# One hybrid decoder layer: the q_b and k_b projections as one 2x2 block product of seven products

## The reference

```
h = rmsnorm(x, mix_norm_g)
u = h @ w_in                      # sections: q/k, v, o of the mLSTM; i, f gates; q, k, v of MoBA
ml_qk, ml_v, ml_o, ml_i, ml_f, mb_q, mb_k, mb_v = split(u)
...
q_b = rmsnorm(heads(mb_q), q_norm_g) * 64 ** -0.5     # per head of 64 columns
k_b = rmsnorm(heads(mb_k), k_norm_g)
h_b = moba_attention(q_b, k_b, v_b)
x = x + concat(h_m, h_b) @ w_out
x = x + moe_ffn(rmsnorm(x), ...)                      # 32 experts, clamped SwiGLU
x = x + sigmoid(rmsnorm(x) @ w_ple_gate) * (p @ w_ple_proj)
```

## Time and profile before

| | us |
|---|---|
| median of 3 runs (lowest, highest) | 1100.59 (1100.36, 1100.77) |
| the profiled execution | 1100.76 |
| its span, first to last instruction | 1099.0 |
| PE busy | 1069.6 (97%) |
| DVE, ACT, POOL busy | 265.5, 143.8, 35.7 |
| moved by DMA | 431.88 MB, mean 393 GB/s |

### The profile page before, as it was taken

One profiled execution on the slowest core, in us unless ns is written; L12 is line 12 of the kernel. 1 busy time (PEld: TensorE's weight loads), 2 busy tenths in 40 slices (PEclk: granted clock), 3 DMA queues, 4 the chain that ended last, 5 costly groups with the idle time before them and its releaser, 6 DMA issues.

```text
span 1099.0 us, 11965 instructions
## 1 busy us (share of the span) xinstructions
PE 1069.6 (97%) x5122; PEld 446.7 (41%) x5122; DVE 265.5 (24%) x535; ACT 143.8 (13%) x284; POOL 35.7 (3%) x52
## 2 busy tenths in 40 slices
PE   9999999999999999999999999998989899999998
PEld 5485563434343434343424333333343343433334
DVE  4285341232121212121211111121211021211122
ACT  4134350100000000000000000000000110000022
POOL 2421200000000000000000000000000000000000
PEclk9999999999999999999999999999999999999999
DMA  9943789999999999999999999999999999999981
GB/s 348 364 174 124 293 332 394 428 414 429 427 426 434 429 436 425 432 432 427 435 431 429 435 425 436 429 429 433 430 431 425 435 428 436 426 431 426 422 341 39
DMA packets 33788, 431.88 MB, mean 393 GB/s; under 512 B 5207, under 2 KB 5727, under 8 KB 16582
## 3 DMA queue, kind: packets, MB, share of 16 engines
q1 hardware_dynamic: 33520, 431.06, 93.2%
q10 hardware_dynamic: 214, 0.04, 0.0%
HBM read 430.04 MB, written 1.06 MB: 392 GB/s over the span
## 4 chain that ended last, share of the span: by engine, by line
PE 75%; DMA 23%; DVE 1%; issue 0%; ACT 0%; DVEq 0%; ACTq 0%
PE hu L1189 28%; DMA ring<-in_w_gate_up 20%; PE po L1219 16%; PE aux L1132 5%; PE aux L1140 3%; DMA ring<-in_w_down 3%; PE hu L792 3%; PE hu L1181 2%; PE hu L1000 2%; PE hu L808 2%; PE hu L798 2%; PE hu L834 1%; PE po L1196 1%; PE aux L1400 1%; PE aux L1165 1%; PE hu L1219 1%
## 5 line engine op out<-in xcount | busy, mean ns | idle before, releaser
L1189 PE MATMUL hu<-ring,num_xg 128*64 128x512 f32 x1920 | 438.4, 604 | 17.1 <-DMA ring<-in_w_gate_up 16.9
L1189 PEld LDWEIGHTS hu<-ring,num_xg 128*64 128x64 f32 x1920 | 132.8, 138 | 302.5 <-issue 273.2
L1219 PE MATMUL po<-ring,arena 128*64 128x512 f32 x976 | 216.2, 594 | 6.3 <-DMA ring<-in_w_down 6.3
L1219 PEld LDWEIGHTS po<-ring,arena 128*64 128x64 f32 x976 | 69.7, 137 | 147.9 <-issue 144.6
L1785 DVE TENSOR_SCALAR arena<-hu 128x512 f32<-128x512 f32 x31 | 21.4, 691 | 428.5 <-PE hu L1189 428.5
L1761 DVE TENSOR_TENSOR arena<-arena,aux 128x512 f32<-128x512 f32 x58 | 37.3, 684 | 131.7 <-PE aux L1140 119.9
L1132 PEld LDWEIGHTS aux<-num_xg,big 128*128 128x128 f32 x512 | 58.4, 192 | 13.0 <-issue 13.0
L1132 PE MATMUL aux<-num_xg,big 128*128 128x128 f32 x512 | 61.4, 278 | 0.0
L1774 DVE TENSOR_SCALAR arena<-iota_s,posm,gates 128x128 f32<-128x128 f32 x64 | 17.9, 342 | 118.2 <-PE po L1219 115.3
L2110 ACT ACTIVATE hu<-arena 128x512 f32<-128x512 f32 x31 | 18.6, 601 | 199.9 <-DVE arena L1785 199.9
L2126 ACT COPY arena<-po 128x512 f32<-128x512 f32 x16 | 9.4, 585 | 221.2 <-PE po L1209 221.2
(11 more groups left out here) (295 smaller groups left out, 670.8 us busy)
## 6 DMA issues: line engine op xcount, KB each, us to landing
ring<-in_w_gate_up SPq DMA_DIRECT2D x44, 4096.0 KB, 34.8
ring<-in_w_down SPq DMA_DIRECT2D x22, 4096.0 KB, 35.0
ring<-in_w_gate_up SPq DMA_DIRECT2D x37, 2048.0 KB, 14.5
ring<-in_w_down SPq DMA_DIRECT2D x14, 2048.0 KB, 15.9
ring<-in_w_in SPq DMA_DIRECT2D x6, 2048.0 KB, 16.2
ring<-in_w_down SPq DMA_DIRECT2D x8, 1024.0 KB, 31.5
ring<-in_w_gate_up SPq DMA_DIRECT2D x6, 1024.0 KB, 6.7
ring<-in_w_out SPq DMA_DIRECT2D x2, 2048.0 KB, 11.5
```

The lines of the kernel that those rows point to most:

```text
L1189: last = mm(hu[n * SLOTS:(n + 1) * SLOTS, 2 * e + b, :], rows_of[:, k, e * SLOTS:(e + 1) * SLOTS], features(w[:, o:o + D], n), start=first ...
L1219: last = mm(bank[n * SLOTS:(n + 1) * SLOTS, :], actT[:, f, h * SLOTS:(h + 1) * SLOTS], w[:, o:o + NB], start=(h == 0 and f == 0), stop=(h ...
```

## The change

Write the tokens as two tiles, and the contraction as two halves. The four blocks q_b and k_b of the two tiles become entries of one 2x2 block product. Its left factor is `raw_block(tt, half)`, its right one `qb_weights(half)`, `kb_weights(half)`. With four sums of row blocks s1 to s4 (POOL, 128x512) and four differences of weight blocks n1 (DVE), n2, n3, n4 (POOL, 128x2048), seven products of 4 steps give all four blocks. All seven read unscaled rows, so the row's factor now comes into the norms of all four blocks. The blocks are finished in the order q_b tile 0, k_b tile 0, k_b tile 1, q_b tile 1 (`BLOCKS`), by adds out of PSUM into `normed`, which ACT and DVE then read in place of the bank. n3 overwrites section 1's first half, n4 the place of n1. The row sums of the later block product (v, o) wait for the end of these products, the `scaled` pair is moved behind the gates, and the load of section 6 waits for n4.

```diff
+        n1 = ring[:, MIX_SLOT, K * S:2 * K * S].rearrange("p (k n) -> p k n", n=NB)
+        n2 = ring[:, CONST_SLOT, W:W + 4 * NB].rearrange("p (k n) -> p k n", n=NB)
+        n4 = n1
...
+        n3 = kb_weights(0)
+        BLOCKS = [0, 2, 3, 1]
...
             def load(n, dst, src):
 
+                if n == 6:
+                    sp.wait_ge(n_ready, 3)
                 if n >= 6:
                     sp.wait_ge(chunk_done, n - 6 + 1)
...
+            pool.wait_ge(hT_act, 8)
+            pool.wait_ge(hT_dve, 2)
+            g.tensor_tensor(s1, raw_block(1, 0), raw_block(1, 1), ALU.add).then_inc(raw_sums, 1)
+            pool.wait_ge(raw_sums, 1)
+            g.tensor_tensor(s2, s1, raw_block(0, 0), ALU.subtract).then_inc(raw_sums, 1)
+            pool.wait_ge(raw_sums, 2)
+            g.tensor_tensor(s4, raw_block(0, 1), s2, ALU.subtract).then_inc(raw_sums, 1)
+            g.tensor_tensor(s3, raw_block(0, 0), raw_block(1, 0), ALU.subtract).then_inc(raw_sums, 1)
+            pool.wait_ge(n1_ready, 1)
+            g.tensor_tensor(n2, kb_weights(1), n1, ALU.subtract).then_inc(n_ready, 1)
+            g.tensor_tensor(n3, kb_weights(1), kb_weights(0), ALU.subtract).then_inc(n_ready, 1)
+            pool.wait_ge(first_ps, 3)
+            pool.wait_ge(n_ready, 1)
+            g.tensor_tensor(n4, qb_weights(1), n2, ALU.subtract).then_inc(n_ready, 1)
...
             pool.wait_ge(xs_ready, TT)
+            pool.wait_ge(chunk_done, 2)
...
-            raw_job(1, range(0, 2))
             pe.wait_ge(gpart_ready, 2)
...
             mm(aux[0:E + H, 0, 0:S], sel_part[:], gpart, start=True, stop=True).then_inc(gate_ps, 1)
-            done_job(1, raw_job(1, range(2, K)))
...
+            wait_chunk(pe, 1)
+            pe.wait_ge(raw_sums, 4)
+            product(pre_r, s4, kb_weights(1), True, True)
+            pe.wait_ge(n1_ready, 1)
+            product(pre_s, s1, n1, True, True).then_inc(first_ps, 1)
+            pe.wait_ge(n_ready, 2)
+            pe.wait_ge(lead_copied, 1)
+            product(sum_p, s2, n2, False, False).then_inc(first_ps, 1)
+            norm_transposes(0)
+            pe.wait_ge(block_ready, 2)
+            product(sum_p, s3, n3, False, False).then_inc(chunk_done, 1)
+            pe.wait_ge(cols_ready, 1)
             pe.wait_ge(xs_ready, TT)
-            job(2)
-            norm_transposes(0)
-            pe.wait_ge(cols_ready, 1)
...
-            job(3)
+            pe.wait_ge(n_ready, 3)
+            pe.wait_ge(block_ready, 3)
+            product(sum_p, raw_block(1, 1), n4, False, True).then_inc(chunk_done, 1)
             norm_transposes(1)
             job(4)
...
-            scaled(1)
+            wait_chunk(dve, 0)
+            wait_chunk(dve, 1)
+            v.tensor_tensor(n1, kb_weights(0), qb_weights(0), ALU.subtract).then_inc(n1_ready, 1)
...
+                v.scalar_tensor_tensor(out=q, in0=q, scalar=stat[:, 16 + i % 2:17 + i % 2], in1=inv, op0=ALU.mult, op1=ALU.mult)                 .then_inc(normed_ready, 1)
...
+            dve.wait_ge(first_ps, 3)
+            dve.wait_ge(pre_sum, 1)
+            v.tensor_tensor(normed[:, 2, :], po[:, 0, :], normed[:, 3, :], ALU.add).then_inc(pre_sum, 1)
+            dve.wait_ge(pre_sum, 2)
+            dve.wait_ge(first_ps, 4)
+            v.tensor_tensor(normed[:, 2, :], normed[:, 2, :], hu[:, 0, :], ALU.add).then_inc(block_ready, 1)
+            scaled(0)
+            scaled(1)
+            dve.wait_ge(chunk_done, 1)
+            v.tensor_tensor(normed[:, 3, :], normed[:, 3, :], hu[:, 0, :], ALU.add).then_inc(block_ready, 1)
```

More of the change, by code:

```diff
@@ L406, in hybrid_layer, with qb_weights, kb_weights, raw_block @@
         t3 = o_weights(0)
+        def qb_weights(half):
+            return slot(0, NB, K)[:, 4 * half:4 * half + 4, :]
+        def kb_weights(half):
+            return slot(1, NB, K)[:, 4 * half:4 * half + 4, :]
+        def raw_block(tt, half):
+            return rawT[:, 4 * half:4 * half + 4, tt * P:(tt + 1) * P]
+        n3 = kb_weights(0)
+        BLOCKS = [0, 2, 3, 1]
         def loads_in(slot, upto):
@@ L464, in wait_job @@
             else:
-                eng.wait_ge(job_ps, sum(not last_of_chunk(i) for i in range(j + 1)))
+                eng.wait_ge(job_ps, sum(not last_of_chunk(i) for i in range(J_VB, j + 1)))
         def selections(pair):
@@ L782, in job @@
                 n = JOB_CHUNK[j]
-                bank = hu[:, j % 2, :]
-                if j >= 2:
+                bank = hu[:, (j + 1) % 2 if j < J_QK else j % 2, :]
+                if j == J_VB + 1:
+                    pe.wait_ge(block_ready, 4)
+                elif j == J_QK:
+                    evacuated(J_VB + 1)
+                elif j == J_QK + 1:
+                    evacuated(J_VB)
+                elif j > J_QK + 1:
                     evacuated(j - 2)
@@ L829, in raw_transposes, with product @@
                         last.then_inc(xT_ps, 1)
-            def raw_job(tt, ks):
+            def product(bank, rows_of, weights, first, last, ks=range(4)):
                 for k in ks:
-                    last = mm(hu[:, tt, :], rawT[:, k, tt * P:(tt + 1) * P], slot(0, NB, K)[:, k, :], start=(k == 0),
-                              stop=(k == K - 1), skip_group_check=True)
-                return last
+                    ins = mm(bank, rows_of[:, k, :], weights[:, k, :], start=(first and k == 0), stop=(last and k == 3),
+                             skip_group_check=True)
+                return ins
+            sum_p, sum_q, sum_r = hu[:, 0, :], hu[:, 1, :], hu[:, 2, :]
+            pre_r, pre_s = po[:, 0, :], po[:, 1, :]
             raw_transposes(0)
@@ L994, in output_transposes @@
                 last.then_inc(hmT_ps, 1)
[L997 to L1004, removed]
             evacuated(J_V - 2)
@@ L1511, in _ @@
             assert n[0] == GATE_STEPS
[L1512 to L1517, removed]
+            dve.wait_ge(first_ps, 3)
[8 more added lines that the diff above has]
+            v.tensor_tensor(normed[:, 3, :], normed[:, 3, :], hu[:, 0, :], ALU.add).then_inc(block_ready, 1)
+            normed_transposed(0)
+            dve.wait_ge(gcol_ps, 1)
+            v.tensor_copy(acol[:].rearrange("p t h -> p (t h)"), hu[:, 2, 0:TT * H]).then_inc(acol_ready, 1)
+            normed_half(1)
+            normed_half(2)
+            normed_transposed(1)
+            normed_half(3)
+            normed_transposed(2)
             normed_transposed(3)
@@ L1921, in _ @@
             row_root(0)
+            act.wait_ge(first_ps, 1)
+            a.copy(normed[:, 0, :], hu[:, 0, :]).then_inc(lead_copied, 1)
             row_root(1)
@@ L1946, in _ @@
+            act.wait_ge(first_ps, 3)
+            a.copy(normed[:, 3, :], po[:, 1, :]).then_inc(pre_sum, 1)
+            act.wait_ge(rstd_ready, TT)
+            block_squares(1)
+            block_roots(1)
+            block_squares(2)
+            block_roots(2)
+            act.wait_ge(chunk_done, 2)
+            a.copy(normed[:, 1, :], hu[:, 0, :]).then_inc(block_ready, 1)
+            block_squares(3)
+            block_roots(3)
             act.wait_ge(gcol_ps, 1)
@@ L1950, in _ @@
                 wait_job(act, J_VB + tt)
-                a.copy(vb[:, tt, :], hu[:, tt, :]).then_inc(vb_ready, 1)
+                a.copy(vb[:, tt, :], hu[:, 1 - tt, :]).then_inc(vb_ready, 1)
             def moba_exp(h):
```

90 lines of the change are left out of this document (46 added, 44 removed).

## The result

| | before | changed |
|---|---|---|
| median of 4 runs, us | 1100.47 (1100.01 to 1100.77) | 1113.17 (1112.39 to 1113.58) |
| ratio | | 1.0114, 95% interval 1.0102 to 1.0125 |
| profiled execution / its span, us | 1100.76 / 1099.0 | 1113.58 / 1111.7 |
| job 4 starts | 39.37 | 52.51 |
| first scores | 54.08 | 67.21 |

The kernel became 12.7 us slower (forecast 1114.1, measured 1113.17). Job 4 starts 13.14 us later, the scores 13.13, the first expert load 12.94, and the span is 12.7 longer: what is lost before job 4 reaches the end nearly whole.

A forecast was written before the change was run, and what follows sets the result against it. TensorE, back to back in the attention stage, was taken as the bound. The saved 3.4 us and the stalls made +11.8, with the clock's 1.7 +13.5: 1114.1 us, range 1111.5 to 1118.

The forecast's parts named there:

- What is removed: TensorE's q/k products: 28 contraction steps for 32, eight matmul instructions of 0.43 us fewer, -3.4 us, wholly on the path.
- One us at job 4 is one us at the end: A TensorE shift at the end of the q/k jobs moves the first expert load and the end by as much.
- The rival in which the weight stream swallows it: Expert stage: the weight stream keeps its times and TensorE's waits there shrink instead; 1100.6 us, chance 0.02.
- the upper end for two SBUF inputs: VectorE instructions with two SBUF tensors are held to the end of GpSimd's current one, up to 4.5 us each.
- the multiply and gate steps 2 and 3: VectorE's norm multiply and second and third gate steps wait for GpSimd's subtractions to end: 25.6, 30.9 and 35.7 us.
- Sizes: Times walked through the q/k products: job 4 at 51.2 us instead of 39.37, +11.8 us before the clock.
- The tenth step: Gate chain on VectorE: its tenth step, for which the transposes of block 0 wait, ends at 41.5 us.
- The pauses: TensorE idles 5.3 us before s2·n2 (25.7 to 31.0) and 7.1 us before block 0's transposes (34.4 to 41.5).
- the first pause: Before s2·n2: time lost to the clock behind it is covered by the gate chain; s2·n2 may end 1.7 us late.
- Clock: Lower granted clock behind the second pause slows s3·n3 on the path: +1.7 us, between 0 and 3.4.
- Behind it: After job 4: job 6's bank wait covered within 0.1 us; output section's weights done near 71, used after 96.
- the last norm multiply: VectorE, beside the later row sums: it has 2 us of room and can lose 3 to a long subtraction.

The follow-up runs named there:

- e9: e8 plus waits so that GpSimd's later two output-section subtractions follow VectorE's normalised heads; 1099.29 us, ratio 0.9986 to the kernel before.
- e1: The changed kernel, but GpSimd waits for the tenth gate step before n2, so no subtraction runs beside the gates; 1114.81 us.
- e2: The changed kernel with n2, n3 and n4 each replaced by two constant fills on GpSimd, which write SBUF and read nothing; 1103.15 us.
- e4: The changed kernel, but s2·n2 waits for n2 alone and s3·n3 for n3; 1114.43 us.
- e5: The changed kernel with 3 and 7 filler products of 128x512 in TensorE's two pauses; 1110.88 us.
- e7: The changed kernel with job 4 on unscaled rows right behind s1·n1 and two norm transposes inside job 5; 1112.88 us.
- e8: The changed kernel with the edits of e6 and e7 together, and s3 summed later; 1105.84 us.
- e3: The changed kernel with 18 filler products of 128x128 ahead of the transposes of block 0; 1113.26 us.
- e11: e7 plus waits so that GpSimd's later two output-section subtractions follow VectorE's normalised heads; 1106.91 us.
- e6: The changed kernel with n2 and n3 on VectorE behind n1, and n4 on GpSimd behind the gate chain; 1106.98 us.

## Why the prediction was right

- *What is removed.* Not measured alone. At full clock a product takes 3.60 to 3.70 us for 8 instructions and the chain's steps kept their 6.87 us for 16, so 8 instructions at 0.43 stand.
- *One us at job 4 is one us at the end.* 13.14 there, 12.94 at the first expert load, 12.7 in the span and in the medians. The rival in which the weight stream swallows it is out.
- *Held instructions: the choice of the upper end for two SBUF inputs.* Right, and this was the step on which the forecast hung. n1 took 3.00 us beside the last row sum for 2.29, and ended at 20.82 (forecast 21.05); in e9, where no row sum stands beside it, it took 2.29; the multiply and gate steps 2 and 3 were held to the ends of n2, n3 and n4, the three that were named. e1 shows that the hold makes the 11 us, e2 which kind is held against what.
- *Sizes.* The tenth step ended at 40.49, not 41.5: I let each GpSimd instruction start behind VectorE's short one, but n4 started 0.04 us before n3's end and took 4.55. The pauses were 2.79 and 6.57 us where 5.3 and 7.1 stood; the first is shorter mainly because s4·kb1 and s1·n1 took 8.76 us where the forecast has 6.9, a slow piece (granted clock 0.66 between 18 and 23 us) that I had not counted. As said of the first pause, it is covered: e4 gives it back without a gain.
- *Clock.* Forecast +1.7, measured 2.05: s3·n3 5.69 us for the 3.64 of e5, which gains 2.2 us of time. The slow transposes (1.08 for 0.60) are covered by VectorE's adds. Without the clock's part job 4 would be 11.1 later (forecast 11.8: the tenth step came 1.0 earlier, the rest behind it 0.3 later). The two errors, -0.7 and +0.35, partly cancel in the sum of 13.14 (forecast 13.5). That the clock's term came so near is in part luck: behind other pauses the same product took from 5.40 to 6.70 us (last section), so up to 1 us more was possible.
- *Behind it.* The output section's weights were done at 71.98 (forecast 71), the last norm multiply was held by 0.28 us (2 us of room), and job 6 started without a wait. All three covered, as forecast.
- *What it did not see.* That these same subtractions hold the heads' normalise. In the kernel before and the changed one they end 6.6 and 4.8 us behind the start of the first scores, early enough, so no term of the sum was wrong; in e7 it is 11.1. The expectations of e7 and e8 left it out and were 7 to 9 and 6 to 7 us off. By the stretch from the scores to the v product the hold, with the slow work behind it, was 5.8 and 5.4 of these; in e7 the slow s3·n3 is 2.6 more.

## What to carry to other kernels

Before work is given to an idle GpSimd, list what VectorE does beside it: here scalings and other elementwise steps with one SBUF input waited for the end of the current GpSimd instruction, and those with two SBUF inputs too where GpSimd reads (a reduction and a reciprocal beside n2 did not); a chain of short steps on the path then pays a whole GpSimd instruction per step. Long GpSimd work goes beside VectorE's stretches on PSUM, by an explicit wait if need be. And when a gain at one point of a stage does not reach the end, look for the same mechanism in the stage behind before giving up the idea.

## What the hardware showed unexpectedly

- The two engines take turns. With GpSimd's instructions queued back to back, VectorE gets one waiting instruction in after each and GpSimd pays for it: n3 took 4.95 us, 0.44 more than the 4.51 of n2, with the multiply (0.75) let in at its start; in e1, with nothing held beside them, n2 and n3 took 4.50 and 4.49. A step of 0.28 let in before n4 cost it 0.04 (4.55). So VectorE's chain advances one step per 4.5 us, neither starved nor free. In e8 two instructions of 0.27 each took 3.25 and 4.61.
- A GpSimd fill of 128x2048 (1.80 us) lets instructions with two SBUF inputs pass and holds those with one (e2).
- The clock behind a pause follows neither the pause's length nor the code alone in these runs. s4·kb1 and s1·n1 are the same instructions behind the same 1.42 to 1.46 us of pause in nine traces: they took 8.66 to 8.80 us in six (the changed kernel, e1, e2, e3, e4, e11) and 7.10 or 7.11 in three (e5, e6, e7). s2·n2 took 3.70 us behind 2.79 of pause (changed kernel) and 5.10 behind 2.74 (e3). s3·n3 took 5.40 behind 2.77 (e11), 6.28 behind 4.42 (e7), 6.70 behind 4.76 (e6), 5.69 behind 6.57 (changed kernel) and 5.71 behind 9.61 (e4). So one trace's slow piece is no fixed price of its pause. What decides was not tried.
